# Rope part of the MLA scores from two rounded products, the queries' rotation two slabs sooner and its split in two steps

## The chip, the cores and the metric

The kernel runs on one core of one Trainium2 chip. The metric is the device time of one execution in microseconds (us); the number given for a kernel is the median of its runs. The engines: TensorE (PE in the views; PEld is its weight load), VectorE (DVE), ScalarE (ACT), GpSimd (POOL) and SyncE (SP), which only issues DMAs.

## What is computed

Two residual blocks on 256 tokens of width 2048, in float32. The first is a LayerNorm and two hybrid layers (MLA attention, a pooling mixer and a convolution mixer side by side), the second one layer with a feed-forward part, three kinds of attention and another feed-forward part. The change touches only the scores of the MLA attention, of which there are 8 heads in each of two layers:

```python
q_nope, q_rope = q[..., :128], q[..., 128:]        # 8 heads, 128 + 64 dimensions
q_rope = apply_rope(q_rope, cos[:, :, None, :], sin[:, :, None, :])
k_rope = apply_rope(k_rope, cos, sin)              # one for all heads
scale = (QK_NOPE_DIM + QK_ROPE_DIM) ** -0.5
s = (jnp.einsum('bqhd,bkhd->bhqk', qn, k_nope)
     + jnp.einsum('bqhr,bkr->bhqk', qr, k_rope)) * scale
```

## The kernel before

Almost all the time goes into products with weights that are read once from HBM, 1 MB to a slab. A slab is loaded into one of four raw buffers; ScalarE writes its rounded high part (`split_high`, L1370, F32R), VectorE subtracts to get the low part (`split_low`, L1777), each in two halves; TensorE then multiplies high by high and low activations in one product of 512 columns (L928) and low by high in one of 256 (L932). Where the activations stand still, it takes three products of 512 columns (L942 to L944).

A hybrid layer is a series of regions, and a slot number counts its slabs: `in_a` 0 to 15, `uq` 16 to 19 (queries, 12 tiles), `uk` 20 (keys, 8 tiles), `uv` 21 and 22 (values), `in_b` 23 to 30, `in_c` 31 and 32, `pool` 33, `in_d` 34 to 46, `out` from 48. The digit behind a region's name is the layer, so `in_b0` is `in_b` of layer 0. `layer_steps` puts the small steps of a layer by hand into slots (`put(slot, step, ...)`), and each engine walks the same list in its own order. For VectorE a slot is: the second half of the low part of the next slab, the slot's steps, the first half of the low part of the slab after that, and the stores of the tiles that TensorE has summed; in `uv` that first half comes ahead of the stores, in `uq` and `uk` in front of `uv` behind them. ScalarE goes likewise with the high parts. A step waits in its queue, and what stands behind it waits too.

The names that matter here:

- `q[:, 8:12, :]` holds the rope part of the queries, two heads to a tile: head h on partitions 0 to 63 and head h + 4 on 64 to 127. SP swaps its halves into `rope_b` by four DMAs (L886, issued behind the load of `in_b` slab 1, when all tiles of `uq` are stored).
- `rope_q` (VectorE, slot 23, L1972 to L1974) multiplies by cosine and sine and adds, three operations of 128 x 1024.
- `rope_k` (VectorE, slot 13) does the same for the one tile of rope keys, which stands on both halves of the partitions. Its sum goes into `kr[:, 0]` on the first half and `kr[:, 1]` on the second (L2108); the other halves were set to zero once (`clear_key`).
- The scores of head h (L1281) are four products in F32 on TensorE: for each block of 128 queries one of `q` with `kn` and one of the rope tile with `kr[:, h // 4]`. The first block sees 128 keys, the second 256. Heads 0 to 7 are at slots 24, 26, 28, 30, 34, 36, 38 and 40, in the middle of the slab.
- Tile 0 of `in_b` is summed in the bank in which `uv`'s first tile was; TensorE waits until VectorE has copied it to `v_mla` (L1874).
- Six small VectorE operations on constants of the second block (L2360 to L2365) stand ahead of `in_b0`.

Of the kernel before, what the change touches and what calls it, by code (L numbers as in the profile page):

```python
# [7 lines left out]
F32 = mybir.dt.float32  # L8
F32R = mybir.dt.float32r
I32 = mybir.dt.int32  # L10
ALU = mybir.AluOpType
# [4 lines left out]
P = 128  # L16
D = 2048
S = 256
# [3 lines left out]
HEADS = 8  # L22
# [203 lines left out]
def layer_steps(layer):  # L226
    steps = {}

    def put(slot, *step):
        for name, first in (("in_a", 0), ("uq", 16), ("uk", 20), ("uv", 21), ("in_b", 23), ("in_c", 31),  # L230
                            ("pool", 33), ("in_d", 34), ("out", 48)):
            r = REG[f"{name}{layer}"]
            if first <= slot < first + r.n:
                steps.setdefault((r.name, slot - first), []).append(step)

    if layer == 0:
        put(7, "tables")
        put(8, "clear_key")
        put(14, "memory_squares", 0)
        put(15, "memory_squares", 1)  # L240
        put(16, "memory_scale")
    put(8, "lat_square", layer)
    put(9, "lat_fold", layer)
    put(9, "lat_sum", layer)
    put(10, "lat_scale", layer)
    put(11, "lat_gain", layer)
    put(12, "lat_split", layer)
    put(13, "rope_k", layer)
    put(23, "rope_q", layer)
    put(13, "silu", layer, 0, 4)  # L250
    put(24, "silu", layer, 4, 8)
    for h, slot in enumerate((24, 26, 28, 30, 34, 36, 38, 40)):
        head_steps(put, layer * HEADS + h, slot, slot + 4)
    for g in range(GROUPS):
        put(24 + 2 * g if g < 3 else 31, "pool", layer, g)
        put(25 + 2 * g, "silu", layer, 8 + g, 9 + g)
        put(33 + 4 * g, "silu", layer, 12 + g, 13 + g)
        put(34 + 4 * g, "conv", layer, g)
    for slot, c in zip((44, 45), MIX_ORDER[layer]):
        put(slot, "mix_split", layer, c)  # L260

    ln = f"ln{layer}"
    put(48 + 4, "shift", ln)
    put(48 + 5, "moments", ln, 0)
    put(48 + 8, "moments", ln, 1)
    put(48 + 12, "moments", ln, 2)
    for n in range(4):
        put(48 + 10 + n, "memory", 8 * layer + 2 * n, 8 * layer + 2 * n + 2)
    put(3, "row", layer)
    for c in range(4):  # L270
        put(4 + c, "residual", layer, c)
    return steps
# [86 lines left out]
def build(nc, t):  # L359

    with ExitStack() as ctx:
        cursor = [(nc.sbuf_base + 31) // 32 * 32]

        def at(name, shape, dt, offset=None):
            size = int(np.prod(shape[1:])) * 4
            if offset is None:
                offset = cursor[0]
                cursor[0] += (size + 31) // 32 * 32
            return nc.alloc_sbuf_tensor_at(name, shape, dt, offset=offset)
# [8 lines left out]
        x = at("x", [P, KT, S], F32)  # L378
        x_tok = at("x_tok", [P, TB, D], F32, x_at)
        memk = at("memk", [P, MEM, S], F32)  # L380
        memv = at("memv", [P, TB, MEM * P], F32)

        work = cursor[0]
# [19 lines left out]
        q = at("q", [P, 12, S], F32, work + 20 * KB)  # L403
        lat_sq = at("lat_sq", [P, 6, S], F32, work + 24 * KB)
        kn = at("kn", [P, HEADS, S], F32, work + 36 * KB)
        kr = at("kr", [P, 2, S], F32, work + 44 * KB)
        mix = at("mix", [P, KT, S], F32, work + 46 * KB)
        feat = at("feat", [P, 24, S], F32, work)
        v_nat = at("v_nat", [P, TB, (FOX + SWA_KV) * P], F32, work + 24 * KB)
# [6 lines left out]
        memh = at("memh", [P, KT // 2, 2 * S], F32R, memh_at)  # L416
        mem_b = at("mem_b", [P, KT // 2, 2 * S], F32, memh_at)
        wide_turn = at("wide_turn", [P, WIDE_TILES, S], F32, memh_at)
        gate = at("gate", [P, S], F32)
        silu_g = at("silu_g", [P, S], F32)  # L420
        up = at("up", [P, S], F32)
        prod = at("prod", [P, S], F32)
# [41 lines left out]
        def sem(name):  # L464
            return ctx.enter_context(nc.semaphore(name))
# [44 lines left out]
        lat_sq_done, lat_sums, lat_var, lat_root, lat_ready = (  # L510
            sem(n) for n in ("lat_sq_done", "lat_sums", "lat_var", "lat_root", "lat_ready"))
        swapped, kr_swapped = sem("swapped"), sem("kr_swapped")
        roped = sem("roped")
        gated = sem("gated")
        pool_ready = sem("pool_ready")

# [257 lines left out]
        def head_spec(n):  # L774

            if n < MLA_ALL:
                h = n % HEADS

                qk = [(q[:, h, :], kn[:, h, :]), (q[:, HEADS + h % 4, :], kr[:, h // 4, :])]
                return "mla", h, qk, [v_mla[:, b, h * P:(h + 1) * P] for b in range(TB)], h  # L780
            m = n - MLA_ALL
            if m < SWA0:
                return "mem", m, [(feat[:, m, :], memk[:, m, :])], [
                    memv[:, b, m * P:(m + 1) * P] for b in range(TB)], m
            if m < FOX0:
                h = m - SWA0
                kv = h // (SWA // SWA_KV)
                return "swa", h, [(feat[:, MEM + SWA_KV + h, :], feat[:, MEM + kv, :])], [
                    v_nat[:, b, kv * P:(kv + 1) * P] for b in range(TB)], 4 + (h - 2) % SWA
            h = m - FOX0  # L790
            k_at = MEM + SWA_KV + SWA + 4 * (h // 2) + h % 2
            return "fox", h, [(feat[:, k_at + 2, :], feat[:, k_at, :])], [
                v_nat[:, b, (SWA_KV + h) * P:(SWA_KV + h + 1) * P] for b in range(TB)], 10 + h
# [131 lines left out]
        def _(eng):  # L925
# [274 lines left out]
            def do(kind, *a):  # L1200
# [63 lines left out]
                elif kind == "scores":  # L1264
# [5 lines left out]
                    if what == "mla":  # L1270
                        layer = n // HEADS
                        eng.wait_ge(stored, REG[f"in_b{layer}"].t0)
                        eng.wait_ge(roped, 2 * layer + 2)
                    else:
                        eng.wait_ge(stored, HEADS_T0)
                        p = {"mem": h // 2, "swa": 3 + h // 2, "fox": 7 + 2 * (h // 2)}[what]
                        eng.wait_ge(pair_done, 2 + p + 1)
# [81 lines left out]
        def _(eng):  # L1359
# [220 lines left out]
            def do(kind, *a):  # L1580
# [61 lines left out]
                elif kind == "lat_square":  # L1642
                    eng.wait_ge(stored, REG[f"in_a{a[0]}"].t0 + KQ + KKV)
                    eng.wait_ge(residual_done, a[0] + 1)
                    eng.activation(lat_sq[:, :, :], lat[:, 0:KQ + KKV, :], ACT.Square).then_inc(lat_sq_done, 1)
                elif kind == "lat_scale":
                    eng.wait_ge(lat_var, a[0] + 1)
                    eng.activation(scale_b[:, :], scale_a[:, :], ACT.Sqrt).then_inc(lat_root, 1)
# [119 lines left out]
        def _(eng):  # L1768
# [208 lines left out]
            def do(kind, *a):  # L1977
# [117 lines left out]
                elif kind == "clear_key":  # L2095
                    for half in range(2):
                        a_ = slice(ROPE * (1 - half), ROPE * (1 - half) + ROPE)
                        ins = eng.memset(kr[a_, half, :], 0.0)
                    step_(ins)
                elif kind == "rope_k":  # L2100
                    layer = a[0]
# [1 line left out]
                    eng.wait_ge(kr_swapped, 64 * (layer + 1))  # L2103
                    step_(eng.tensor_tensor(lat[:, 6, :], lat[:, 6, :], cos[:, :], ALU.mult))
                    step_(eng.tensor_tensor(lat[:, 7, :], lat[:, 7, :], sin[:, :], ALU.mult))
                    for half in range(2):
                        a = slice(ROPE * half, ROPE * half + ROPE)
                        ins = eng.tensor_tensor(kr[a, half, :], lat[a, 6, :], lat[a, 7, :], ALU.add)  # L2108
                    ins.then_inc(roped, 1)
                    eng.wait_ge(roped, 2 * layer + 1)  # L2110
                elif kind == "rope_q":
                    layer = a[0]
                    wide = [v[:, :].unsqueeze(1).to_broadcast([P, HEADS // 2, S]) for v in (cos, sin)]
                    eng.wait_ge(swapped, 64 * (layer + 1))
                    rotate(q[:, HEADS:, :], rope_b[:, :, :], *wide, q[:, HEADS:, :], rope_b[:, :, :], 2 * layer + 2)
                elif kind == "conv":
                    layer, g = a

# [235 lines left out]
            def between(name):  # L2354
                if name == "in_a0":
                    eng.memset(unit[:, :], 1.0).then_inc(unit_there, 1)
                    layer_norm("emb", None)
                if name == "in_b0":
                    for g in ("fox_q", "swa_q", "mem_q"):
                        step_(eng.tensor_scalar(p_(g), p_(g), HEAD_SCALE, None, ALU.mult))  # L2360
                    step_(eng.tensor_scalar(neg_sink[:, :], p_("sinks", 0, SWA), -1.0, None, ALU.mult))
# [173 lines left out]
```

## Time and profile before

| | |
|---|---|
| median of 3 runs | 2531.89 us (2531.88 to 2533.27) |
| the profiled execution's own time | 2532.84 us |
| its span in the record | 2531.1 us |
| TensorE, VectorE, ScalarE busy | 99%, 73%, 52% |
| DMA | 480.84 MB, 190 GB/s in the mean |
| granted clock of TensorE | 1.00 |

The span is the time between the first and the last recorded instruction, and all positions below are microseconds from its start. A busy engine may still not be at its peak: the products overlap, so what one of them costs in a stream is the distance between two starts, not its duration. Several products in a row by the same line and on the same tiles stand in one row of the timeline, with their count. In square brackets at the end of a row is how long its engine had been idle and which instruction ended that.

### The profile page before, as it was taken

The page shows a single profiled execution, that of the slowest core. Times are in us where ns is not written, and L with a number is a line of the kernel's source. Part 1 is how long each engine was busy: PE and PEld are TensorE (multiplying, and loading weights), DVE is VectorE, ACT ScalarE, POOL GpSimd, SP SyncE. Part 2 cuts the span into 40 slices and gives each one's busy share as a digit, 9 for nine tenths or more (in the row PEclk, how much of TensorE's full clock was granted, in tenths as well). Part 3 has the DMA queues.
Part 4 walks back from the last instruction along what each step waited for, and adds up shares of the span by engine and source line. Part 5 has one row for each costly group of instructions (what it writes and reads, how often), then busy time and mean ns, then how long its engine had stood idle before and what let it go on. Part 6 is the DMA issues. An engine that isn't in the chain of part 4 may idle for free.

```text
span 2531.1 us, 33093 instructions
## 1 busy us (share of the span) xinstructions
PE 2517.0 (99%) x12088; PEld 2110.2 (83%) x12088; DVE 1851.9 (73%) x2983; ACT 1313.4 (52%) x1885; POOL 25.5 (1%) x24
## 2 busy tenths in 40 slices
PE   8999999999999999999999999999999999999999
PEld 6888888888888888888888887888888888888888
DVE  8777658777658777677777786678777767777766
ACT  6665565565566444444444555765544444444443
POOL 4000000000000000000000000000000000000000
PEclk9999999999999999999999999999999999999999
DMA  7554556554555555555555554444555555555554
GB/s 302 202 191 171 198 185 234 169 193 168 199 184 189 193 198 186 196 184 201 197 191 183 190 202 151 148 158 173 186 199 190 192 184 198 200 196 188 197 183 150
DMA packets 71231, 480.84 MB, mean 190 GB/s; under 512 B 8000, under 2 KB 10688, under 8 KB 17216
## 3 DMA queue, kind: packets, MB, share of 16 engines
q1 hardware_dynamic: 71104, 479.16, 53.6%
q8 instruction: 78, 1.28, 0.2%
q14 instruction: 49, 0.40, 0.0%
HBM read 475.72 MB, written 2.10 MB: 189 GB/s over the span
## 4 chain that ended last, share of the span: by engine, by line
PE 83%; DVE 1%; ACT 1%; issue 0%; ACTq 0%; DVEq 0%
PE acc L942 12%; PE acc L944 12%; PE acc L943 12%; PE score L942 10%; PE score L944 10%; PE score L943 10%; PE acc L928 9%; PE acc L932 4%; PE score L1281 1%; PE score L928 1%; PE head_ps L1306 0%; PE score L932 0%; PE turn_ps L1290 0%; DVE low L1777 0%; PE head_ps L1307 0%
## 5 line engine op out<-in xcount | busy, mean ns | idle before, releaser
L1777 DVE TENSOR_TENSOR low<-raw,high 128x1024 fp32r<-128x1024 f32 (+2 forms) x912 | 1079.2, 1188 | 468.6 <-ACT high L1370 460.5
L1370 ACT ACTIVATE high<-raw 128x1024 fp32r<-128x1024 f32 (+2 forms) x912 | 935.0, 1028 | 846.9 <-PE acc L944 436.3
L928 PE MATMUL acc<-xs,high 128*128 128x512 f32 x1184 | 396.8, 398 | 1.5 <-DVE xs L2312 1.3
L942 PE MATMUL acc<-high,xs 128*128 128x512 f32 x928 | 366.3, 395 | 0.3 <-DVE scale_a L1870 0.3
L944 PE MATMUL acc<-low,xs 128*128 128x512 f32 x928 | 361.6, 390 | 0.0
L943 PE MATMUL acc<-high,xs 128*128 128x512 f32 x928 | 361.1, 389 | 0.0
L932 PE MATMUL acc<-xs,low 128*128 128x256 f32 x1184 | 297.6, 279 | 0.0
L942 PE MATMUL score<-high,xs 128*128 128x512 f32 x736 | 286.4, 389 | 0.0
L944 PE MATMUL score<-low,xs 128*128 128x512 f32 x736 | 286.3, 389 | 0.0
L943 PE MATMUL score<-high,xs 128*128 128x512 f32 x736 | 286.3, 389 | 0.0
L928 PEld LDWEIGHTS acc<-xs,high 128*128 128x128 f32 x1184 | 219.4, 188 | 50.2 <-DVE xs L2312 2.0
L1824 DVE STREAM_TRANSPOSE unit_turn<-unit_prod 32x128 f32<-32x128 f32 x704 | 212.8, 302 | 9.8
L932 PEld LDWEIGHTS acc<-xs,low 128*128 128x128 f32 x1184 | 211.9, 188 | 4.2
L944 PEld LDWEIGHTS acc<-low,xs 128*128 128x128 f32 x928 | 174.2, 188 | 36.9
L942 PEld LDWEIGHTS acc<-high,xs 128*128 128x128 f32 x928 | 174.2, 188 | 36.5 <-issue 1.0
L943 PEld LDWEIGHTS acc<-high,xs 128*128 128x128 f32 x928 | 174.3, 188 | 35.5
L944 PEld LDWEIGHTS score<-low,xs 128*128 128x128 f32 x736 | 138.2, 188 | 28.8
L942 PEld LDWEIGHTS score<-high,xs 128*128 128x128 f32 x736 | 138.2, 188 | 28.7
L943 PEld LDWEIGHTS score<-high,xs 128*128 128x128 f32 x736 | 138.2, 188 | 28.5
L942 PE MATMUL score<-high,hidden 128*128 128x512 f32 x352 | 136.9, 389 | 0.0
L943 PE MATMUL score<-high,hidden 128*128 128x512 f32 x352 | 136.9, 389 | 0.0
L944 PE MATMUL score<-low,hidden 128*128 128x512 f32 x352 | 136.9, 389 | 0.0
(398 smaller groups left out, 3177.1 us busy)
## 6 DMA issues: line engine op xcount, KB each, us to landing
raw<-w_up_dram SPq DMA_DIRECT2D x176, 1024.0 KB, 4.8
raw<-w_in_dram SPq DMA_DIRECT2D x76, 1024.0 KB, 4.8
raw<-w_wide_dram SPq DMA_DIRECT2D x75, 1024.0 KB, 4.8
raw<-w_out_dram SPq DMA_DIRECT2D x32, 1024.0 KB, 4.8
raw<-w_heads_dram SPq DMA_DIRECT2D x20, 1024.0 KB, 4.8
raw<-w_mixout_dram SPq DMA_DIRECT2D x16, 1024.0 KB, 4.8
raw<-w_mem_dram SPq DMA_DIRECT2D x8, 1024.0 KB, 4.8
raw<-w_first_dram SPq DMA_DIRECT2D x8, 1024.0 KB, 4.8
```

The costliest lines, as they stand in the source:

```text
L928: return eng.matmul(bank_, hi, moving, start=start, stop=False)
L932: return eng.matmul(bank_[:, 0:S], lo, moving[:, 0:S], start=False, stop=stop)
L942: eng.matmul(bank_, xh, hi, start=start, stop=False)
L943: eng.matmul(bank_, xl, hi, start=False, stop=False)
L944: return eng.matmul(bank_, xh, lo, start=False, stop=stop)
L1281: last = eng.matmul(score[n % 2][:, b, 0:w], qc[:, b * P:(b + 1) * P], kc[:, 0:w], start=(m == 0), stop=(m == len(qk) - 1))
L1370: eng.activation(high[:, s % SPLIT, to:to + n * P], raw[:, s % RAW, at_:at_ + n * P], ACT.Copy).then_inc((highs_a, highs_b)[piece], 1)
L1777: eng.tensor_tensor(low[:, s % SPLIT, w], raw[:, s % RAW, at_:at_ + n * P], high[:, s % SPLIT, w].bitcast(F32), ALU.subtract).then_inc((lo ...
L1824: ins = eng.transpose(to[QUAD * j:QUAD * (j + 1), n, :, :, :], from_[QUAD * n:QUAD * (n + 1), j, :, :, :])
```

## The change

The rope product of a head in F32 becomes two in F32R, with the same stationary operand each. That operand has the rounded (high) rope queries of a head on 64 partitions and their remainder (low) on the other 64; `rope_first` holds it for heads 0 to 3, `rope_late` for heads 4 to 7. The moving operand of the first product is `key_high`, the rounded rope keys on both halves, and that of the second `key_low`, the keys' remainder on the half with the high queries and zero on the other. `rope_k` therefore sums into `lat`, rounds into `key_high` and subtracts into `key_low`. `rope_q` goes from slot 23 to 21. A new step `rope_split` makes the stacked operand, half 0 in slot 22 and half 1 in slot 27: ScalarE copies 64 x 1024 (the high part), and VectorE, when that is there, subtracts 64 x 1024 from one half of the partitions to the other. The first score of a half waits for it (`rope_low`). The six operations on constants go from ahead of `in_b0` to ahead of `out1`.

```diff
--- before.py
+++ after.py
@@ -246,7 +246,9 @@
     put(11, "lat_gain", layer)
     put(12, "lat_split", layer)
     put(13, "rope_k", layer)
-    put(23, "rope_q", layer)
+    put(21, "rope_q", layer)
+    put(22, "rope_split", layer, 0)
+    put(27, "rope_split", layer, 1)
     put(13, "silu", layer, 0, 4)
     put(24, "silu", layer, 4, 8)
     for h, slot in enumerate((24, 26, 28, 30, 34, 36, 38, 40)):
@@ -378,6 +380,7 @@
         x = at("x", [P, KT, S], F32)
         x_tok = at("x_tok", [P, TB, D], F32, x_at)
         memk = at("memk", [P, MEM, S], F32)
+        rope_first = at("rope_first", [P, HEADS // 2, S], F32R, cursor[0] - 4 * S * MEM)
         memv = at("memv", [P, TB, MEM * P], F32)
 
         work = cursor[0]
@@ -403,7 +406,8 @@
         q = at("q", [P, 12, S], F32, work + 20 * KB)
         lat_sq = at("lat_sq", [P, 6, S], F32, work + 24 * KB)
         kn = at("kn", [P, HEADS, S], F32, work + 36 * KB)
-        kr = at("kr", [P, 2, S], F32, work + 44 * KB)
+        key_low = at("key_low", [P, 2, S], F32R, work + 44 * KB)
+        rope_late = at("rope_late", [P, HEADS // 2, S], F32R, work + 16 * KB)
         mix = at("mix", [P, KT, S], F32, work + 46 * KB)
         feat = at("feat", [P, 24, S], F32, work)
         v_nat = at("v_nat", [P, TB, (FOX + SWA_KV) * P], F32, work + 24 * KB)
@@ -416,7 +420,7 @@
         memh = at("memh", [P, KT // 2, 2 * S], F32R, memh_at)
         mem_b = at("mem_b", [P, KT // 2, 2 * S], F32, memh_at)
         wide_turn = at("wide_turn", [P, WIDE_TILES, S], F32, memh_at)
-        gate = at("gate", [P, S], F32)
+        key_high = at("key_high", [P, S], F32R)
         silu_g = at("silu_g", [P, S], F32)
         up = at("up", [P, S], F32)
         prod = at("prod", [P, S], F32)
@@ -510,7 +514,7 @@
         lat_sq_done, lat_sums, lat_var, lat_root, lat_ready = (
             sem(n) for n in ("lat_sq_done", "lat_sums", "lat_var", "lat_root", "lat_ready"))
         swapped, kr_swapped = sem("swapped"), sem("kr_swapped")
-        roped = sem("roped")
+        roped, rope_high, rope_low = sem("roped"), sem("rope_high"), sem("rope_low")
         gated = sem("gated")
         pool_ready = sem("pool_ready")
 
@@ -776,7 +780,8 @@
             if n < MLA_ALL:
                 h = n % HEADS
 
-                qk = [(q[:, h, :], kn[:, h, :]), (q[:, HEADS + h % 4, :], kr[:, h // 4, :])]
+                rope = (rope_first, rope_late)[h // 4][:, h % 4, :]
+                qk = [(q[:, h, :], kn[:, h, :]), (rope, key_high[:, :]), (rope, key_low[:, h // 4, :])]
                 return "mla", h, qk, [v_mla[:, b, h * P:(h + 1) * P] for b in range(TB)], h
             m = n - MLA_ALL
             if m < SWA0:
@@ -1270,7 +1275,7 @@
                     if what == "mla":
                         layer = n // HEADS
                         eng.wait_ge(stored, REG[f"in_b{layer}"].t0)
-                        eng.wait_ge(roped, 2 * layer + 2)
+                        eng.wait_ge(rope_low, 2 * layer + h // 4 + 1)
                     else:
                         eng.wait_ge(stored, HEADS_T0)
                         p = {"mem": h // 2, "swa": 3 + h // 2, "fox": 7 + 2 * (h // 2)}[what]
@@ -1643,6 +1648,12 @@
                     eng.wait_ge(stored, REG[f"in_a{a[0]}"].t0 + KQ + KKV)
                     eng.wait_ge(residual_done, a[0] + 1)
                     eng.activation(lat_sq[:, :, :], lat[:, 0:KQ + KKV, :], ACT.Square).then_inc(lat_sq_done, 1)
+                elif kind == "rope_split":
+                    layer, half = a
+                    eng.wait_ge(roped, 2 * layer + 2)
+                    to = (rope_first, rope_late)[half]
+                    a_ = slice(ROPE * half, ROPE * half + ROPE)
+                    eng.activation(to[a_, :, :], q[a_, HEADS:, :], ACT.Copy).then_inc(rope_high, 1)
                 elif kind == "lat_scale":
                     eng.wait_ge(lat_var, a[0] + 1)
                     eng.activation(scale_b[:, :], scale_a[:, :], ACT.Sqrt).then_inc(lat_root, 1)
@@ -2095,7 +2106,7 @@
                 elif kind == "clear_key":
                     for half in range(2):
                         a_ = slice(ROPE * (1 - half), ROPE * (1 - half) + ROPE)
-                        ins = eng.memset(kr[a_, half, :], 0.0)
+                        ins = eng.memset(key_low[a_, half, :].bitcast(F32), 0.0)
                     step_(ins)
                 elif kind == "rope_k":
                     layer = a[0]
@@ -2103,9 +2114,11 @@
                     eng.wait_ge(kr_swapped, 64 * (layer + 1))
                     step_(eng.tensor_tensor(lat[:, 6, :], lat[:, 6, :], cos[:, :], ALU.mult))
                     step_(eng.tensor_tensor(lat[:, 7, :], lat[:, 7, :], sin[:, :], ALU.mult))
+                    step_(eng.tensor_tensor(lat[:, 6, :], lat[:, 6, :], lat[:, 7, :], ALU.add))
+                    step_(eng.tensor_copy(key_high[:, :], lat[:, 6, :]))
                     for half in range(2):
                         a = slice(ROPE * half, ROPE * half + ROPE)
-                        ins = eng.tensor_tensor(kr[a, half, :], lat[a, 6, :], lat[a, 7, :], ALU.add)
+                        ins = eng.tensor_tensor(key_low[a, half, :], lat[a, 6, :], key_high[a, :].bitcast(F32), ALU.subtract)
                     ins.then_inc(roped, 1)
                     eng.wait_ge(roped, 2 * layer + 1)
                 elif kind == "rope_q":
@@ -2113,6 +2126,13 @@
                     wide = [v[:, :].unsqueeze(1).to_broadcast([P, HEADS // 2, S]) for v in (cos, sin)]
                     eng.wait_ge(swapped, 64 * (layer + 1))
                     rotate(q[:, HEADS:, :], rope_b[:, :, :], *wide, q[:, HEADS:, :], rope_b[:, :, :], 2 * layer + 2)
+                elif kind == "rope_split":
+                    layer, half = a
+                    to = (rope_first, rope_late)[half]
+                    a_, other = (slice(ROPE * n, ROPE * n + ROPE) for n in (half, 1 - half))
+                    eng.wait_ge(rope_high, 2 * layer + half + 1)
+                    eng.tensor_tensor(to[other, :, :], q[a_, HEADS:, :], to[a_, :, :].bitcast(F32), ALU.subtract)\
+                        .then_inc(rope_low, 1)
                 elif kind == "conv":
                     layer, g = a
 
@@ -2355,7 +2375,7 @@
                 if name == "in_a0":
                     eng.memset(unit[:, :], 1.0).then_inc(unit_there, 1)
                     layer_norm("emb", None)
-                if name == "in_b0":
+                if name == "out1":
                     for g in ("fox_q", "swa_q", "mem_q"):
                         step_(eng.tensor_scalar(p_(g), p_(g), HEAD_SCALE, None, ALU.mult))
                     step_(eng.tensor_scalar(neg_sink[:, :], p_("sinks", 0, SWA), -1.0, None, ALU.mult))
```

## Rows read from the trace of the kernel before

**Rows 1.** The page: busy time by engine; TensorE's granted clock by slice.

```profile
PE 2517.0 (99%) x12088; PEld 2110.2 (83%) x12088; DVE 1851.9 (73%) x2983; ACT 1313.4 (52%) x1885; POOL 25.5 (1%) x24
...
PEclk9999999999999999999999999999999999999999
```

**Rows 2.** TensorE's waits: who, for whom, us in total, times, longest.

```profile
PE sums L1351 <- DMA x_tok<-x_dram: 6.2, 1, 6.2
```

**Rows 3.** Timeline, TensorE, head 0: start us, us, instruction, shape, count.

```profile
146.95 0.39 PE L1281 MATMUL score<-kr,q 128*128 128x128 f32 x2
147.18 0.60 PE L1281 MATMUL score<-kn,q 128*128 128x256 f32 x2
147.61 0.59 PE L1281 MATMUL score<-kr,q 128*128 128x256 f32 x2
...
148.27 0.28 PE L932 MATMUL acc<-xs,low 128*128 128x256 f32 x1
```

**Rows 4.** Timeline, TensorE, start of in_b0.

```profile
138.40 1.98 PE L928 MATMUL acc<-xs,high 128*128 128x512 f32 x8
```

**Rows 5.** Timeline, TensorE, the pool products of layer 0.

```profile
202.63 0.28 PE L1145 MATMUL sums<-pooled,high 128*128 128x256 f32 x1
...
203.23 0.28 PE L1147 MATMUL sums<-pooled,low 128*128 128x256 f32 x1
203.73 0.38 PE L1145 MATMUL acc<-pooled,high 128*128 128x256 f32 x1 [0.21 <-DVE branch L1901]
```

**Rows 6.** Timeline, TensorE, the cumulative sums and what follows.

```profile
1554.81 0.95 PE L1248 MATMUL head_ps<-fz,par 128*128 128x6 f32 x8
1555.69 0.60 PE L1251 MATMUL head_ps<-par,fz 128*6 128x256 f32 x2
```

**Rows 7.** Timeline, VectorE, slots 21 to 23 of layer 0.

```profile
135.52 1.22 DVE L1777 TENSOR_TENSOR low<-raw,high 128x1024 fp32r<-128x1024 f32 x1 [0.17 <-ACT high L1370]
136.67 0.75 DVE L1874 COPY v_mla<-acc 128x256 f32<-128x256 f32 x2
...
140.26 0.52 DVE L2360 TENSOR_SCALAR par<-par 128x1 f32<-128x1 f32 x3
...
141.45 1.22 DVE L1777 TENSOR_TENSOR low<-raw,high 128x1024 fp32r<-128x1024 f32 x1
142.58 1.22 DVE L1972 TENSOR_TENSOR q<-q,cos 128x1024 f32<-128x1024 f32 x1
...
146.35 1.22 DVE L1777 TENSOR_TENSOR low<-raw,high 128x1024 fp32r<-128x1024 f32 x1
```

**Rows 8.** Tile rope_b: the swapping DMAs, both layers.

```profile
L886 SPq DMA_DIRECT2D rope_b<-q x8: 512/590/1432, 128.3 to 509.3; - x8
...
DMA to landing us min/median/max: 3.2/3.4/3.6
```

**Rows 9.** Timeline, VectorE, slot 21 of layer 1.

```profile
515.91 0.75 DVE L1874 COPY v_mla<-acc 128x256 f32<-128x256 f32 x2
```

**Rows 10.** Timeline, TensorE, start of in_b1.

```profile
517.67 1.98 PE L928 MATMUL acc<-xs,high 128*128 128x512 f32 x8
```

**Rows 11.** Timeline, ScalarE, a high part of 128 x 1024 in slot 23.

```profile
138.88 1.06 ACT L1370 ACTIVATE high<-raw 128x1024 fp32r<-128x1024 f32 x1
```

**Rows 12.** Timeline, VectorE, slot 13 of layer 0: rotation of the keys.

```profile
99.42 0.85 DVE L2108 TENSOR_TENSOR kr<-lat 64x256 f32<-64x256 f32 x2
100.31 1.22 DVE L1777 TENSOR_TENSOR low<-raw,high 128x1024 fp32r<-128x1024 f32 x1
```

**Rows 13.** Timeline, VectorE, slot 27 of layer 0.

```profile
170.19 1.23 DVE L1777 TENSOR_TENSOR low<-raw,high 128x1024 fp32r<-128x1024 f32 x1 [1.93 <-ACT high L1370]
```

**Rows 14.** Timeline, VectorE, start of out1.

```profile
670.02 2.35 DVE L1777 TENSOR_TENSOR low<-raw,high 128x1024 fp32r<-128x1024 f32 x2
```

**Rows 15.** Timeline, TensorE, start of out1.

```profile
666.11 0.39 PE L942 MATMUL acc<-high,mixs 128*128 128x512 f32 x1
```

**Rows 16.** Timeline, TensorE, first products of the record.

```profile
6.21 6.68 PE L1351 MATMUL sums<-x_tok 128*128 128x512 f32 x8 [6.21 <-DMA x_tok<-x_dram]
```

## The prediction

> **What bounds the kernel now.** I read the page's first part: TensorE is busy for 2517.0 of 2531.1 us, VectorE for 73%, ScalarE for 52% [rows 1]. Of the 14 us left, 6.2 are the wait for the first input, the first line in the list of TensorE's waits [rows 2]; so all waits behind it come to under 8 us. TensorE is therefore the bound all the way, but "waits for nobody" is not "nobody is close to making it wait": a step on VectorE that is moved in front of something TensorE needs costs as soon as it is longer than the slack at that place. So two prices decide: what the rope products take on TensorE, and how much slack there is where the rotation now goes. The records of the other engines in the stretches around the attention steps (125 to 175 us for layer 0, 505 to 555 us for layer 1) give the second.
>
> **Rope products on TensorE (removed and added).** An F32 product stands as two records, an F32R product as one. In head 0 the rope product over 128 keys starts at 146.95 and its successor at 147.18: 0.23 us. The one over 256 keys starts at 147.61; behind it comes a weight product of 512 columns, and at 148.27 its L932 partner. Products of 512 columns follow each other by 0.23 (eight in 1.98, the last 0.39 long [rows 4]), so the rope product ended at 148.04: 0.43 us [rows 3]. Together 0.66 us a head, 16 heads. The new products are F32R. With 256 columns there is a row for exactly this, six in a stream, each with weights of its own: 202.63 to 203.23 is five steps, 0.12 each [rows 5]. Two take 0.24, and a pair of 512 and 256 columns, of which a slab has sixteen, 0.35. For 128 moving columns in F32R the trace has no row. Bounds: from below half of 0.12, i.e. 0.06, if it goes by columns alone; from above 0.23, what a 128-column F32 product takes. Between them lies the pace at which weights of 128 columns follow each other when there is almost nothing to stream: eight records with 6 moving columns from 1554.81 to 1555.69, 0.11 each [rows 6]. I take 0.115, as the rows nearest in form (own weights each time) say: two take 0.23. Per head 0.24 + 0.23 = 0.47 instead of 0.66, so 0.19 saved, times 16 = **3.0 us off TensorE**. By the lower bound the saving is 0.66 - 0.24 - 0.12 = 0.30 a head, 4.8 us; by the upper one 0.66 - 0.24 - 0.46 = -0.04, a loss of 0.6 us.
>
> The rows show 0.66 us for 384 columns in F32 and 0.12 for 256 in F32R. The Trainium skill, "FP8 and Floating Point Precision", section TensorE Precision Notes, says that true FP32 makes four passes and reduced precision FP32 needs none of the extra ones; as an estimate by that page, 384 columns at 2.4 GHz would be 0.64 us in F32 and 2 x 0.16 = 0.32 us for the two new products, 5.1 us saved in all. Its four passes agree with the row of F32. What it leaves out is the weight load: "TensorE: Matmul & The Clock Gate", section LDWEIGHTS (loading the stationary operand), gives P/1.2, 107 ns for 128 columns, and the 0.11 of the row agrees; under that floor a 128-column product can't use its shorter stream.
>
> **The rotation, two slabs sooner (moved).** VectorE's order in a slab's slot is: second half of the next slab's low parts, the slot's steps, first half of the low parts of the slab after that, stores. In slot 21 (`uv0`, k = 0) the steps were empty, so behind the second half of `uv` slab 1, which ended at 135.35, and 0.17 of waiting came the 1024-wide split at 135.52, which is the first half of slab 0 of `in_b0`, and then the two copies into `v_mla` at 136.67. The first copy frees the bank in which `in_b0` tile 0 is summed, and TensorE waits for both, the low half and that copy. They were there at about 137.05 (136.67 and half of 0.75), TensorE came at 138.40 [rows 4, 7]: slack 1.3 us. Now the rotation stands in between. Its three operations run from 142.58, and the split behind them starts at 146.35: 3.77 us [rows 7]. Its inputs are there: the four swapping DMAs are issued from 128.3 on, 0.6 us each, so by 130.7, and land 3.2 to 3.6 us after issue, by 134, and SP's queue order isn't touched [rows 8]. VectorE would begin at about 135.27 (a next instruction starts some 0.08 before the end of the last), start the split at 139.04 instead of 135.52, so 3.52 later, and end the first copy at 140.6. A restart after a wait for VectorE cost about 0.1 (the product at 203.73 has 0.38 where its likes have 0.28) [rows 5]. TensorE stands from 138.40 to 140.6 and loses 0.1 or 0.2 more: 2.4 us. Layer 1 repeats it: copies at 515.91, TensorE at 517.67; the first copy would end at 515.91 + 0.38 + 3.52 = 519.8, a stand of 2.1 and 0.1 to 0.2 more, 2.3 us [rows 9, 10]. **Added: 4.7 us on the path.** Hardly anything can give it back, since TensorE's waits after the first come to under 8 us in the whole record [rows 1, 2]. What is queued on VectorE behind the moved step is the low half, the two copies, then the second low half (ready then at 142.1; TensorE wants it half a slab, 8 x 0.35 = 2.8 us, after its start, 143.4: no second stand).
>
> **The split, in two steps.** Half 0 stands in slot 22. ScalarE waits there for the rotation (139.04), copies 64 x 1024, about the 1.05 of its 128 x 1024 copies, and behind it are queued the high half of `in_b0` slab 1 and two copies of values [rows 11]. They end about 141.9; the high half is done at 141.1 and VectorE comes for it at 143.1. VectorE pays 1.22, what 1024 columns on 128 partitions take, since its time goes by columns: two operations of 64 x 256 take 0.85 [rows 7, 12]; slab 1's low half is then ready at about 144.4 and TensorE wants it at 140.7 + 5.56 = 146.2. Hidden, 1.8 us of slack; where the rotation used to stand VectorE is 3.77 us lighter, and in layer 0 another 1.2. Half 1 stands in slot 27: there VectorE had been waiting 1.93 us for ScalarE's high half when it began at 170.19 [rows 13]. ScalarE's copy puts that high half off by 1.05, VectorE's subtraction ends about 0.1 behind it, so the low half of slab 6 begins at about 171.4. TensorE comes to slab 6 at 138.40 plus six slabs of 5.56 and three score blocks of at least 1.1, 175.1 or later [rows 3, 4]. Slack over 2 us. Nothing on the path. If that cover were gone it would be 1.2 us a layer.
>
> **Rope of the keys.** One more 128 x 256 add and one cast in slot 13: about 0.42 + 0.29 and two semaphore steps, 0.8 us. Behind them stands the first half of slab 15, from 100.3 to 101.5, then to 102.3 [rows 12]. Counted back from 138.40, two slabs of `uv` are 24 x 0.23, `uk` 16 x 0.35, the four of `uq` 48 x 0.35 and slab 15 itself 16 x 0.35: TensorE begins it at about 105. Hidden.
>
> **Constants.** Six small VectorE operations, 140.26 to 141.45, 1.2 us [rows 7], leave the end of slot 22 and go ahead of `out1`, where they push, among others, the second half of `out1`'s slab 1, from 670.02 to 671.2, then to 672.4 [rows 14]. TensorE begins `out1` at 666.11 and needs that half after 36 products of 0.23, at 674.4 [rows 15]. Nothing.
>
> Sum: -3.0 + 4.7 = +1.7 us on a span of 2531.1. The profiled execution's own time was 2532.84, the median of the runs shown 2531.89; the difference belongs to the execution, so I add to the median: **2533.6 us**.
>
> **Rivals.** (a) A 128-column F32R product costs what the F32 one does. For it: no row shows one faster. Against it: the 256-column ones show no such cost. The saving turns into -0.6: 2531.9 + 0.6 + 4.7 = 2537.2. (b) It goes by columns alone, 0.06: -4.8 + 4.7, 2531.8. Against it: the 0.11 of [rows 6]. (c) No stand: VectorE gets to slot 21's steps earlier or the rotation delays the copy by less than the 1.3 us of slack. Against it: VectorE shows 0.17 us of idle time before that split and none behind it up to the copies [rows 7]. It would leave the saving alone: 2528.9. (d) Slower: TensorE's pace falls after the stand in front of `in_b`. In every slice of the record the granted clock has the digit 9, the level of 2.4 GHz [rows 1], but all its waits after the start together are under 8 us, and a single one would now be 2.2. The first products of the record, eight of 512 columns in F32, take 6.68 us, 0.83 each [rows 16], where by the 0.43 / 2 of one 256-column record [rows 3] they would take 0.43; that is the price of one slow beginning, 8 x 0.4 = 3.2 us. At two stands this is 6.4 more: 2540.0. It decides from the point where a stand of 2.2 us is enough for a lower clock, which no row shows. The Trainium skill, "TensorE: Matmul & The Clock Gate", section HAM oscillation, tells of such falls between bursts; nothing in this trace bears it out.
>
> **How the numbers follow.** Forecast 0.50; (a) 0.24; (b) 0.08; (c) 0.08; (d) 0.06; 0.02 for savings beyond every bound, 0.02 for other losses. The range 2530.8 to 2538.2 holds the forecast, (a) and (b), 0.82. What a measurement can tell from no change is 0.2%, 5.1 us, so the limits are 2526.8 and 2537.0. (a) stands on the upper limit and is split in two. Faster 0.02, slower 0.12 + 0.06 + 0.02 = 0.20, same 0.78.
>
> **What would show it.** Right: the rope records number one for each product, 0.11 to 0.12 apart; TensorE has a wait of about 2.2 us at its first product of `in_b0` and `in_b1` (ending near 140.6 and 520.7, where the second holds 0.9 us of shift, 2.4 less eight heads' 0.19), for VectorE's `v_mla` copy or low half; no other wait appears at the slots 22 to 28 and at `out1`. Wrong: records 0.2 apart at 128 columns (a); no wait at `in_b` (c); a granted clock of 0.5 behind it (d); or a wait for the swapping DMA, which I put at none.

## The result, and the profile of the changed kernel

The changed kernel takes 2536.32 us (median of 20 runs, 2533.92 to 2537.87), the kernel before 2532.28 (20 runs, 2531.80 to 2533.27): a ratio of 1.0017, 95% interval 1.0011 to 1.0023. It is 4.0 us slower, a loss that is sure but small, within the 0.2% named above. The forecast was 2533.6, the range 2530.8 to 2538.2.

The profiled execution has a span of 2536.0 us against 2531.1. First the page, busy time by engine and the granted clock in 40 slices:

```profile
PE 2517.2 (99%) x12088; PEld 2110.1 (83%) x12088; DVE 1859.1 (73%) x2991; ACT 1318.1 (52%) x1889; POOL 24.5 (1%) x24
...
PEclk9999999999999999999999999999999999999999
```

TensorE has as many records as before and 0.2 us more busy time, though its rope products have become cheaper [rows 1]; what takes the difference is the third item below. The slices, 63 us each, show nothing; what they average away comes below. TensorE's waits (who, for whom, total, times, longest):

```profile
PE sums L1356 <- DMA x_tok<-x_dram: 6.4, 1, 6.4
PE acc L933 <- DVE v_mla L1885: 4.2, 2, 2.1
```

Besides the wait for the first input [rows 2] there is one new entry of weight, and it is the one forecast: the first product of `in_b`, twice, for the copy into `v_mla`. The timeline of TensorE has both places, with the first score block behind each:

```profile
140.71 3.00 PE L933 MATMUL acc<-xs,high 128*128 128x512 f32 x8 [2.11 <-DVE v_mla L1885]
...
150.80 0.38 PE L1286 MATMUL score<-kn,q 128*128 128x128 f32 x2
150.94 0.31 PE L1286 MATMUL score<-key_high,rope_first 128*128 128x128 f32 x1
151.08 0.27 PE L1286 MATMUL score<-key_low,rope_first 128*128 128x128 f32 x1
151.19 0.65 PE L1286 MATMUL score<-kn,q 128*128 128x256 f32 x2
151.49 0.47 PE L1286 MATMUL score<-key_high,rope_first 128*128 128x256 f32 x1
151.79 0.28 PE L1286 MATMUL score<-key_low,rope_first 128*128 128x256 f32 x1
151.91 0.39 PE L933 MATMUL acc<-xs,high 128*128 128x512 f32 x1
...
522.41 2.50 PE L933 MATMUL acc<-xs,high 128*128 128x512 f32 x8 [2.11 <-DVE v_mla L1885]
```

Three readings. `in_b0` starts at 140.71 instead of 138.40 [rows 4]; 0.04 of that lies ahead of the stand (the stretch in which TensorE stands idle in front of `in_b`), so 2.27 come from it. `in_b1` starts at 522.41 instead of 517.67 [rows 10]: 2.48 us of shift are carried there, and 2.27 are new. And eight products of 512 columns take 3.00 or 2.50 us from the first start to the last end, where they took 1.98. Comparing start by start through the whole record, the shift jumps at these two places and nowhere else by more than 0.3, but for 0.4 at 19 us, in the opening (from 0.2 ahead of before to 0.2 behind it), where TensorE waited 0.47 us for a low part. Then it falls by 0.187 us at each of the 16 heads: 3.0 us.

That slower pace behind the two stands is the third item. The windows view behind the two stands (stretch, length, busy time and instructions of the five engines, granted clock, DMA share, GB/s):

```profile
140.71:141.60 0.89, 0.89 (x4) 0.76 (x5) 0.89 (x2) 0.89 (x4) 0.00 (x0) 1.00 0.00 0
141.60:145.20 3.60, 3.60 (x15) 3.11 (x14) 3.54 (x5) 0.98 (x2) 0.00 (x0) 0.53 0.49 166
145.20:150.00 4.80, 4.80 (x30) 4.15 (x29) 3.35 (x5) 2.88 (x4) 0.00 (x0) 1.00 0.74 268
522.41:523.80 1.39, 1.39 (x6) 1.17 (x7) 1.39 (x2) 1.39 (x4) 0.00 (x0) 1.00 0.00 0
523.80:527.40 3.60, 3.60 (x15) 3.17 (x14) 3.54 (x6) 1.18 (x2) 0.00 (x0) 0.53 0.68 232
527.40:532.00 4.60, 4.60 (x29) 4.03 (x28) 3.08 (x4) 2.53 (x4) 0.00 (x0) 1.00 0.67 255
```

The granted clock is still 1.00 for 0.9 us behind the first stand and for 1.4 us behind the second. Then it is down to 0.5, the level of 1.2 GHz, for 3.4 us: the two stretches of 3.60 us have a mean of 0.53, so all but 0.2 us of each is at 0.5. The first holds fifteen records; the next 4.8 us at 2.4 GHz hold thirty. The cost can be read off the kernel's own rows. From the first product of `in_b` to the first score product behind it, before needs 138.40 to 146.73, 8.33 us, and the same in layer 1. After needs 140.71 to 150.80, 10.09, and 522.41 to 532.42, 10.01. Of the 1.76 and 1.68 more, about 0.13 are the restart after a wait (the experiment `two_thirds` shows it by itself), the other 1.6 and 1.55 are the clock.

The sum of after: 0.04 + 2.27 + 1.76 + 2.27 + 1.68 - 3.0 = 5.0, measured 4.9 from span to span. Only the clock was not in the forecast's sum.

The fall doesn't come in every execution, and this is why the runs of this kernel lie 4 us apart where those of before lie within 1.5. They fall in groups: one at 2533.92 with a mean clock of 1.000 over the whole run, then nine from 2535.49 to 2536.00, one at 2536.64, nine from 2537.07 to 2537.87, all these at 0.999. The distances, 1.9 and 1.7 between the middles of the groups, are near the price of one such stretch, so I read the groups as none, one and both. The profiled execution, 2537.74, has both in its record and belongs to the last. The mean clock alone can't tell them apart, since one stretch and two are both 0.999 when rounded, and the lower clock can come elsewhere too: two of the 28 runs of before beside the later experiments have 0.999 as well, at 2532.75 and 2533.42.

The steps that should be hidden are so. VectorE around the moved rotation, layer 0:

```profile
134.12 1.29 DVE L1788 TENSOR_TENSOR low<-raw,high 128x512 fp32r<-128x512 f32 x2
135.33 1.22 DVE L1983 TENSOR_TENSOR q<-q,cos 128x1024 f32<-128x1024 f32 x1
...
137.84 1.22 DVE L1985 TENSOR_TENSOR q<-q,rope_b 128x1024 f32<-128x1024 f32 x1
139.10 1.22 DVE L1788 TENSOR_TENSOR low<-raw,high 128x1024 fp32r<-128x1024 f32 x1
140.24 0.75 DVE L1885 COPY v_mla<-acc 128x256 f32<-128x256 f32 x2
140.91 1.22 DVE L1788 TENSOR_TENSOR low<-raw,high 128x1024 fp32r<-128x1024 f32 x1
142.15 1.22 DVE L2134 TENSOR_TENSOR rope_first<-q,rope_first 64x1024 fp32r<-64x1024 f32 x1
```

The split began at 135.52 and the copies at 136.67 before [rows 7]; now it is 139.10 and 140.24, 3.6 us later, behind three operations that wait for nobody. The slack of 1.3 us swallows what it can, and 2.27 remain. The subtraction of half 0 at 142.15 takes 1.22, as said, and is waited for by no one. The other displaced steps, in the keys' slot 13, slot 27 and `out1`:

```profile
99.44 0.42 DVE L2117 TENSOR_TENSOR lat<-lat 128x256 f32<-128x256 f32 x1
99.90 0.29 DVE L2118 CAST key_high<-lat 128x256 fp32r<-128x256 f32 x1
...
101.12 1.22 DVE L1788 TENSOR_TENSOR low<-raw,high 128x1024 fp32r<-128x1024 f32 x1
...
173.98 1.22 DVE L2134 TENSOR_TENSOR rope_late<-q,rope_late 64x1024 fp32r<-64x1024 f32 x1 [2.06 <-ACT rope_late L1656]
175.23 1.23 DVE L1788 TENSOR_TENSOR low<-raw,high 128x1024 fp32r<-128x1024 f32 x1
...
673.92 2.35 DVE L2219 TENSOR_TENSOR mixs<-mix,mixs 128x1024 fp32r<-128x1024 f32 x2
676.19 3.49 DVE L1788 TENSOR_TENSOR low<-raw,high 128x1024 fp32r<-128x1024 f32 x3
```

In slot 13 the low part comes at 101.12 instead of 100.31, 0.8 later [rows 12]; in slot 27 VectorE waits 2.06 us for ScalarE's copy, where it waited 1.93 for the high half [rows 13]. TensorE's waits have no entry that belongs to any of them.

### The profile page after: what moved, and what is told of

Its sections match the earlier page's. It is cut to its first block, busy times and chain, and to the rows that moved or that the text cites. A ratio compares the mean times of both kernels' runs of the same rounds, so it can differ in the third digit from the quotient of the medians.

```text
span 2536.0 us, 33104 instructions
## 1 busy us (share of the span) xinstructions
PE 2517.2 (99%) x12088; PEld 2110.1 (83%) x12088; DVE 1859.1 (73%) x2991; ACT 1318.1 (52%) x1889; POOL 24.5 (1%) x24
## 4 chain that ended last, share of the span: by engine, by line
PE 83%; DVE 1%; ACT 1%; issue 0%; ACTq 0%; DVEq 0%
PE acc L947 12%; PE acc L949 12%; PE acc L948 12%; PE score L947 10%; PE score L949 10%; PE score L948 10%; PE acc L933 9%; PE acc L937 4%; PE score L933 1%; PE score L1286 1%; PE head_ps L1311 0%; PE score L937 0%; DVE low L1788 0%; PE turn_ps L1295 0%; PE head_ps L1312 0%
```

## The experiments

Theory, from the reading of after: the change saves 3.0 us by its products, pays 2.4 us twice for the place of the rotation, and up to 1.6 us twice for a lower clock that the two stands bring with them. Rivals: the products' stacked form rather than the stand slows what is behind it; a stand of any length brings the clock down; the late split, the rope of the keys or the constants cost something that the comparison of starts hides. Each run has before beside it on the same chip: 2532.10 us (35 runs, chip 7) for `rot_only`, `rot_22`, `two_thirds` and `rot_23`, 2532.17 (28 runs, chip 4) for the other four.

### The rotation alone (`rot_only`)

To the kernel before:

```diff
-    put(23, "rope_q", layer)
+    put(21, "rope_q", layer)
```

> The kernel before with one edit: the rotation in slot 21 instead of 23; products and constants as before. Theory (stand plus clock): TensorE stands 2.1 us at the start of in_b in both layers, restart included 2.4 each, and a granted clock of 0.5 behind each stand costs some 1.5 more: +4.8 to +7.8, 2537 to 2540 us, and no rope saving. Rival (the products or the split cost the time, not the place): no stand, 2532.3.

Measured: 2537.35 us (2536.39 to 2540.23, 11 runs), ratio 1.0023, interval 1.0014 to 1.0032. TensorE's waits:

```profile
PE acc L928 <- DVE v_mla L1874: 4.2, 2, 2.1
```

and the windows behind the stand in layer 0 and in layer 1:

```profile
140.00:146.00 6.00, 5.97 (x34) 5.20 (x35) 5.83 (x13) 1.12 (x2) 0.00 (x0) 1.00 0.51 178
521.50:526.00 4.50, 4.46 (x17) 3.74 (x18) 4.38 (x6) 0.00 (x0) 0.00 (x0) 0.62 0.41 135
```

With the old products and nothing else changed, the same two stands and the same fall of the clock: the new products have no part in either. In this execution the clock fell only in layer 1. From the first product of `in_b` to the first score it is 8.48 us in layer 0 and 10.10 in layer 1, against 8.33 in before; the whole price of the clock thus stands inside one trace. The 11 runs show three groups again: six from 2536.39 to 2537.35 at a clock of 1.000, two at 2538.25 and 2538.38, three from 2539.98 to 2540.23. The first group is before plus two stands, 2532.1 + 4.8 = 2536.9, and the steps to the others are 1.4 and 1.7.

### The rotation in slot 22, the split in 23 (`rot_22`)

To the changed kernel:

```diff
-    put(21, "rope_q", layer)
-    put(22, "rope_split", layer, 0)
+    put(22, "rope_q", layer)
+    put(23, "rope_split", layer, 0)
```

> The changed kernel with the rotation in slot 22 and the first half of the split in 23, so that in_b's first low half and the value copies go ahead of the rotation. Theory: no stand at in_b, no lower clock, the products' 0.187 us a head stay: 2532.3 - 3.0 = 2529.3 us. The second low half of in_b slab 1 has only about 0.5 us of slack. Rival (the rotation costs wherever it stands before in_b): a stand moves to slab 1 and the time is 2532 or more.

Measured: 2529.45 us (2529.15 to 2530.08; one run of 12 with twice that time was left out), ratio 0.9989, interval 0.9981 to 0.9998; span 2527.7, clock 1.000. In the timeline, first TensorE at the start of `in_b0`, then VectorE:

```profile
137.58 0.39 PE L949 MATMUL score<-low,lats 128*128 128x512 f32 x1
137.80 1.98 PE L933 MATMUL acc<-xs,high 128*128 128x512 f32 x8
```

```profile
136.11 0.75 DVE L1885 COPY v_mla<-acc 128x256 f32<-128x256 f32 x2
136.77 1.22 DVE L1788 TENSOR_TENSOR low<-raw,high 128x1024 fp32r<-128x1024 f32 x1
137.90 1.22 DVE L1983 TENSOR_TENSOR q<-q,cos 128x1024 f32<-128x1024 f32 x1
```

The copies end before TensorE comes, the rotation stands behind them, and `in_b0` begins without a bracket: no wait. What is left of the change is its saving, 2.65 us by the medians (3.0 by the products), so the late split, the keys and the constants together cost at most some tenths. With `split_24`, which can't be told from it, this kernel is the fastest of the study: slot 21 was one too early.

Its record also has, in the opening, a wait of TensorE about as long as the stands:

```profile
13.16 1.06 PE L1347 MATMUL score<-par,z 128*128 128x128 f32 x8 [1.98 <-DVE z L2292]
```

The granted clock is 1.00 from 11 to 20 us all the same.

### A shorter stand (`two_thirds`)

To `rot_22`: two of the rotation's operations in slot 21, the third in 22.

```diff
-    put(22, "rope_q", layer)
+    put(21, "rope_q", layer)
+    put(22, "rope_sum", layer)
...
-                    rotate(q[:, HEADS:, :], rope_b[:, :, :], *wide, q[:, HEADS:, :], rope_b[:, :, :], 2 * layer + 2)
+                    step_(eng.tensor_tensor(q[:, HEADS:, :], q[:, HEADS:, :], wide[0], ALU.mult))
+                    step_(eng.tensor_tensor(rope_b[:, :, :], rope_b[:, :, :], wide[1], ALU.mult))
+                elif kind == "rope_sum":
+                    eng.tensor_tensor(q[:, HEADS:, :], q[:, HEADS:, :], rope_b[:, :, :], ALU.add).then_inc(roped, 1)
+                    eng.wait_ge(roped, 2 * a[0] + 2)
```

> The changed kernel with two of the rotation's three operations in slot 21, the sum in 22 and the first half of the split in 23. Theory: the stand is 2.5 - 0.17 - 1.3 = 1.0 us in each layer, 1.1 with the restart. If the clock falls after any stand of TensorE: 2532.3 - 3.0 + 2.2 + 3.0 = 2534.5 and a granted clock of 0.5 behind it. If it takes a longer one: 2531.5 and a clock of 1.00.

Measured: 2531.68 us (2531.25 to 2532.22, 11 runs), ratio 0.9998, interval 0.9989 to 1.0007. TensorE's timeline, the start of `in_b0` and the score behind it:

```profile
139.42 2.11 PE L934 MATMUL acc<-xs,high 128*128 128x512 f32 x8 [0.83 <-DVE v_mla L1886]
...
147.88 0.38 PE L1287 MATMUL score<-kn,q 128*128 128x128 f32 x2
```

and the windows behind both stands:

```profile
139.40:150.00 10.60, 10.58 (x62) 9.36 (x63) 10.41 (x14) 7.19 (x8) 0.00 (x0) 1.00 0.57 204
518.30:530.00 11.70, 11.69 (x68) 10.32 (x69) 11.40 (x18) 5.88 (x7) 0.00 (x0) 1.00 0.59 198
```

A stand of 0.8 us leaves the clock at 1.00, here and in all 11 runs (mean clock 1.000). What it costs is plain: the start is 1.02 later and the stretch up to the score 8.46 instead of 8.33, so 1.15 us, twice, and -3.0 + 2.3 from 2532.1 is 2531.4. So a stand in front of `in_b` doesn't bring the clock down whatever its length.

### A longer stand (`longer_stand`)

To the changed kernel, one more operation of 128 x 1024 behind the rotation:

```diff
+                    step_(eng.tensor_tensor(rope_b[:, :, :], rope_b[:, :, :], wide[1], ALU.mult))
```

> The changed kernel with one more operation of 128 x 1024 (1.25 us) behind the rotation in slot 21, whose result nothing reads. Theory: the stand at in_b grows from 2.1 to 3.35 us in each layer, and the lower clock then follows both stands in all or nearly all runs at about 1.6 us each: 2532.1 - 3.0 + 2 x 3.5 + 3.2 = 2539.3 us, the runs closer together than the 4 us of the changed kernel. If the lower clock has nothing to do with the stand's length: falls as often as before, runs in three groups from 2536 to 2539.3.

Measured: 2541.02 us (2539.43 to 2541.34, 6 runs), ratio 1.0033, interval 1.0021 to 1.0045. TensorE's waits:

```profile
PE acc L933 <- DVE v_mla L1885: 6.7, 2, 3.4
```

and the windows behind the stands:

```profile
141.40:144.80 3.40, 3.24 (x8) 2.60 (x9) 3.34 (x5) 0.77 (x1) 0.00 (x0) 0.50 0.28 48
144.80:150.00 5.20, 5.20 (x34) 4.63 (x33) 4.12 (x6) 2.14 (x3) 0.00 (x0) 1.00 0.71 263
523.70:530.50 6.80, 6.18 (x19) 5.24 (x20) 6.28 (x9) 1.82 (x4) 0.00 (x0) 0.50 0.43 154
530.50:536.00 5.50, 5.50 (x35) 4.85 (x34) 3.21 (x4) 2.83 (x5) 0.00 (x0) 1.00 0.53 191
```

The stand grows by the operation's 1.25 us, as expected, and now no run is without the lower clock (0.998 or 0.999 in all six). In this record it began while TensorE still stood: the stretches at 0.5 start at 141.4 and 523.7, the first products at 141.56 and 524.32. The miss is 1.7 us: in layer 1 the lower clock lasted 6.8 us, twice as long as in layer 0. From the start of `in_b` to the score it is 9.94 us in layer 0 and 11.34 in layer 1, that is 1.5 and 2.9 for the clock against the 8.46 of `two_thirds`. Why one stretch is twice the other stays open.

### The rotation where it was (`rot_23`)

To `rot_22`:

```diff
-    put(22, "rope_q", layer)
+    put(23, "rope_q", layer)
```

> The changed kernel with the rotation left in slot 23 and the first half of the split behind it in the same slot. Theory: rotation, ScalarE's copy (1.05) and VectorE's subtraction (1.22) end about 147.4 in layer 0 and 526.7 in layer 1, 0.7 us after TensorE comes to the first head's scores: a stand of 0.7 to 0.8 us there in each layer, 2532.3 - 3.0 + 1.5 = 2530.8 us. Rival (the scores hide it): 2529.3.

Measured: 2531.47 us (2531.16 to 2532.47, 11 runs), ratio 0.9997, interval 0.9989 to 1.0006. From TensorE's waits:

```profile
PE score L1286 <- DVE rope_first L2134: 1.6, 2, 0.8
```

So the rotation can't just stay in slot 23 either: with the split's 1.22 us behind it, the first score waits 0.8 us in each layer. By the times this costs 2.0 us against `rot_22`, and from `in_b0`'s first product to the first score it is 9.31 us instead of 8.33, so 1.0 a layer and not the 0.7 to 0.8 expected: the 0.81 of idle time and some 0.2 that the restart adds. In slot 21 it stands in the way of `in_b`, in 23 it is late for the scores, in 22 it is neither.

### Four more 128-column products a head (`extra_128`)

To `rot_22`, in the first query block of each MLA head:

```diff
+                            for _ in range(4 if what == "mla" and b == 0 and m == 2 else 0):
+                                eng.matmul(score[n % 2][:, b, 0:w], qc[:, b * P:(b + 1) * P], kc[:, 0:w], start=False, stop=False)
```

> The kernel with the rotation in slot 22, and on the first query block of each head the product with key_low over 128 keys four times more (64 products; the scores are wrong by these). It measures the disputed price. At the pace of weights, 0.11 to 0.12 each: 2529.4 + 7.0 to 7.7 = 2536.8 us. By columns alone, 0.06: 2533.2. At the price of an F32 product, 0.23: 2544.

Measured: 2536.53 us (2536.32 to 2536.97, 11 runs), ratio 1.0017. Against `rot_22` that is 7.08 us for 64 products, 0.111 each (7.04 against `split_24`, which ran on the same chip). The timeline of a head:

```profile
146.46 0.61 PE L1287 MATMUL score<-key_low,rope_first 128*128 128x128 f32 x4
146.91 0.28 PE L1288 MATMUL score<-key_low,rope_first 128*128 128x128 f32 x1
147.02 0.65 PE L1288 MATMUL score<-kn,q 128*128 128x256 f32 x2
```

From 146.46 to 146.91 four products start: 0.112 each, hardly less than the 0.12 of one with 256 columns. An F32R product of 128 columns costs neither its columns alone (0.06, rival b) nor what the F32 one costs (0.23, rival a), but the 0.11 of the products with 6 columns [rows 6]. That the weights set this pace fits both rows; no run changes the weights alone.

### The late split three slots sooner (`split_24`)

To `rot_22`:

```diff
-    put(27, "rope_split", layer, 1)
+    put(24, "rope_split", layer, 1)
```

> The kernel with the rotation in slot 22, and the second half of the split in slot 24 instead of 27, one slab behind the first. Theory: VectorE and ScalarE have room there, 2529.4 us, no difference. Rival: slot 24 has the pool step and the first head's scores too, and the low half of in_b slab 3 comes late: a stand of TensorE near slab 3, up to 1.2 us a layer, 2531.8.

Measured: 2529.49 us (2529.09 to 2530.47, 11 runs), ratio 0.9989, interval 0.9980 to 0.9998: no difference from `rot_22`. The place of half 1 is free, at least from slot 24 to 27.

### The constants alone (`constants_only`)

To the kernel before:

```diff
-                if name == "in_b0":
+                if name == "out1":
```

> The kernel before with the six operations on constants ahead of out1, nothing else. Theory: hidden at both places, 2532.1 us. Rival: they delay out1's low half by more than its slack of 2 us: up to +1.2.

Measured: 2532.47 us (2531.83 to 2532.97, 11 runs), ratio 1.0000, interval 0.9991 to 1.0009. Nothing, as forecast. But its record and that of `split_24` show the lower clock where the change has no part, in the opening. First the wait ahead of it in `constants_only`, then the windows of `constants_only` and of `split_24`:

```profile
17.19 0.69 PE L928 MATMUL acc<-xs,high 128*128 128x512 f32 x1 [0.94 <-DVE xs L2312]
```

```profile
17.32:20.73 3.41, 3.41 (x11) 2.93 (x12) 3.32 (x5) 2.36 (x5) 0.98 (x1) 0.50 1.01 408
```

```profile
17.55:20.94 3.39, 3.39 (x13) 2.90 (x12) 3.25 (x6) 2.83 (x6) 1.89 (x2) 0.50 1.01 408
```

This wait is the last of three (1.29, 0.73 and 0.94 us in `constants_only`) that stand within 5.1 us. The other eight records have the three too and stay at 1.00, `rot_22` among them with 1.98, 0.73 and 0.82. So neither the length of one wait nor their sum alone decides. The runs of `rot_22`, `rot_23`, `split_24` and `constants_only` with a mean clock of 0.999 lie 0.4 to 1.1 us above the median of the others.

## Why the prediction was right, and where not

- **The bound.** Right. TensorE has no slack, and every microsecond of stand appears in the time.
- **Rope products, -3.0.** Right: 16 x 0.187 = 3.0. The term without a row of its own, 128 moving columns in F32R, was taken from the 0.11 of products with 6 columns [rows 6] as 0.115 and measured 0.111 and 0.112. The trace of before had a nearer row, the transposes over 128 columns in the opening (L1342): eight in 1.07 us, the last 0.27 long, so 0.11 apart. Rivals (a) and (b) are out. The Trainium skill, "TensorE: Matmul & The Clock Gate", section LDWEIGHTS (loading the stationary operand), gives P/1.2 ns for a weight load, by which 128 columns are an estimated 107 ns; the 0.111 agrees, while the records of single weight loads in the trace are 0.19 us long and overlap. The 5.1 us that the prediction estimated by the Trainium skill, "FP8 and Floating Point Precision", section TensorE Precision Notes, from columns alone, did not come: 3.0 did.
- **The rotation in slot 21, +4.7.** Right. Foretold were stands of 2.2 and 2.1 and 0.1 to 0.2 of restart, 2.4 and 2.3 in all, ending at 140.6; measured 2.27 + 0.13 in each layer, and the first product at 140.71. In layer 1 it came at 522.41 instead of the foretold 520.7, because the clock behind the first stand had added 1.6 by then. It rested on three rows: where VectorE's copies stood, when TensorE came, and how long the three operations run. Rival (c), no stand, is out. `rot_only` gives the same stands with the rotation moved alone.
- **The four steps costed at nothing.** Right: `rot_22`, `split_24` and `constants_only` leave together a few tenths.
- **The sum, +1.7.** It holds for a run in which the clock doesn't fall: the one run of after at a mean clock of 1.000 took 2533.92, and 2532.3 + 1.7 is 2534.0. That is a single run. It fails for the other nineteen, because it took TensorE's pace behind a stand as unchanged. That is rival (d), which had 0.06. The mechanism is real, and both its inputs were off. Its condition: a stand of 2.1 us is enough in some 28 of the 40 stands of after (two a run, by the groups of run times: nine runs with both, ten with one) and in 8 of 22 in `rot_only`. Its price: 3.2 us a stand was taken from the first eight products of the record [rows 16]; measured 1.5 to 1.6, since the lower clock ends again after 3.4 us. Forecast plus the measured clock, 2533.6 + 0.7 x 2 x 1.6 = 2535.8, lies by the measured 2536.3; the rest is mostly the base, 2531.89 from three runs where twenty give 2532.28. The Trainium skill's "TensorE: Matmul & The Clock Gate", section HAM oscillation, tells of an engine that falls to half its clock over a wait and begins its next burst there; the 0.5 behind the stands bears it out. The waits of its example are longer than the 2.1 us that were often enough here.
- **The range held by luck.** Its upper part, up to 2538.2, was there for rival (a), the dear 128-column product, and (a) is refuted. 2536.3 lies in it because the lower clock costs about what (a) would have. The one rival that came true had no place in the range.
- **Why the chance was too small.** I gave (d) 0.06 because nothing in the trace of before bore it out, the 9 in every slice of the clock [rows 1] included. That was no evidence against it: the page of after has a 9 in every slice too, with two falls in its record, and the trace of before has no wait over 0.9 us behind the opening, so it couldn't show what one does. A rival whose condition the old trace never meets deserves its price in the range and more than 0.06.

What stays open: why some stands of 2.1 us bring the clock down and others, at the same place in the same kernel, don't, why three short waits in the opening do so in two records of ten, and why the clock once stayed down twice as long.

## What to carry to other kernels

In a kernel whose TensorE never waits, look up for each moved step what VectorE or ScalarE frees for TensorE right behind its new place, and compare the step's length with the slack there; one slot later can be the whole difference between 4 us lost and 2.7 won. Where a stand is unavoidable, keep it short: in front of `in_b` 0.8 us cost its own length and the restart, 2.1 us up to 1.6 more, 3.4 us 1.5 to 2.9 more. And price a small product by a row of its own size, not by its columns: under 256 columns these F32R products get hardly cheaper.

## What the runs showed of the hardware

- TensorE's granted clock after a stand in front of an otherwise dense stream: 0.8 us at `in_b`, 1.00 in the record and, by the mean clock of the runs, in all 22 stands; 2.1 us, 0.5 in the record behind three of four, and behind some 36 of 62 counted by the groups of run times; 3.4 us, 0.5 in the record behind both, and no run of six without it. It falls between 0.7 us ahead of the restart and 1.5 us behind it, and comes back after 3.4 us, once after 6.8.
- In the opening, where three waits of 0.6 to 2.0, 0.7 and 0.8 to 1.0 us follow each other, the granted clock is 0.5 for 3.4 us right behind the last in two records of ten.
- A product of 128 columns in F32R with a weight load of its own starts 0.111 us after the last, one of 256 columns 0.12, one of 512 columns 0.23.
- VectorE's subtraction of 64 x 1024 from one half of the partitions to the other takes 1.22 us, the same as one of 128 x 1024.
